# Summing four conditioning groups early, over row blocks on VectorE, instead of late on TensorE, in a hybrid decoder block

## The reference, cut to what matters

```python
c_act = jax.nn.silu(c)                                    # (1, 1024)
mod = (c_act @ w_ada + b_ada)[:, None, :]                 # w_ada is (1024, 6144)
sh1, sc1, g1, sh2, sc2, g2 = jnp.split(mod, 6, axis=-1)
h = rmsnorm(x, norm1_w) * (1.0 + sc1) + sh1
proj = h @ w_in
cq, k, v, ki, wi, rq, rf, ri, rg, gates = jnp.split(proj, IN_POINTS, axis=-1)
cq = rmsnorm(cq, q_norm_w)
q, qi = cq @ w_uq, cq @ w_uq_idx
attn = dsa_attention(q, k, v, qi, ki, wi, rel_bias)       # 256 keys a query, chosen by index scores
rec = hgrn2(rq, rf, ri, lower_bounds)                     # gated linear recurrence, 4 heads
rec = rmsnorm(rec, rec_norm_w) * jax.nn.silu(rg)
g_attn, g_rec = jnp.split(jax.nn.sigmoid(gates), 2, axis=-1)
mixed = (g_attn * (attn @ w_branch_attn) + g_rec * (rec @ w_branch_rec)) @ w_out
x = x + g1 * mixed
h2 = rmsnorm(x, norm2_w) * (1.0 + sc2) + sh2
x = x + g2 * (silu(h2 @ w_ffn_gate) * (h2 @ w_ffn_up)) @ w_ffn_down
return rmsnorm(x, final_norm_w)
```

## Time and profile before

| what | value |
|---|---|
| median of 3 runs | 1865.67 us (1864.72 to 1866.22) |
| the profiled execution's own time | 1867.28 us |
| its span (first to last instruction) | 1865.5 us |
| PE busy | 1727.7 us, 93% of the span |
| DVE busy | 822.1 us, 44% |
| ACT busy | 605.7 us, 32% |
| POOL busy | 280.9 us, 15% |
| PE's share of the chain that ended last | 75%, "issue" 13% |

### The profile page before, as it was taken

One profiled execution on the slowest core, in us unless ns is written; L12 is line 12 of the kernel. 1 busy time (PEld: TensorE's weight loads), 2 busy tenths in 40 slices (PEclk: granted clock), 3 DMA queues, 4 the chain that ended last, 5 costly groups with the idle time before them and its releaser, 6 DMA issues.

```text
span 1865.5 us, 21187 instructions
## 1 busy us (share of the span) xinstructions
PE 1727.7 (93%) x8203; PEld 1374.0 (74%) x8203; DVE 822.1 (44%) x1382; ACT 605.7 (32%) x874; POOL 280.9 (15%) x215
## 2 busy tenths in 40 slices
PE   4997899999999988999999969999999999999996
PEld 3772487888888833787877757888888888787875
DVE  4215899865574742565343462111111111234343
ACT  5235421556565412557012332111111111222232
POOL 2300122434354200223000220000000000001001
PEclk8999999999999998999999989999999999999998
DMA  9101211321122384000434311111111111342231
GB/s 323 38 26 40 62 46 46 106 64 47 56 66 65 109 319 142 1 1 5 155 118 181 130 68 46 45 45 56 45 45 52 49 45 45 124 155 93 90 124 57
DMA packets 128479, 155.28 MB, mean 83 GB/s; under 512 B 8347, under 2 KB 90390, under 8 KB 128406
## 3 DMA queue, kind: packets, MB, share of 16 engines
q1 hardware_dynamic: 119766, 135.42, 22.4%
q10 hardware_dynamic: 8064, 16.78, 2.4%
q0 software_dynamic: 576, 2.10, 0.3%
HBM read 132.77 MB, written 20.98 MB: 82 GB/s over the span
## 4 chain that ended last, share of the span: by engine, by line
PE 75%; issue 13%; DVE 4%; ACT 3%; DMA 2%; POOL 2%; SPq 1%; POOLq 0%; DVEq 0%; ACTq 0%
PE pp L496 19%; PE pp L497 18%; PE pp L498 18%; PE pp L1197 6%; PE pp L1203 3%; PE pp L1218 2%; PE pp L1386 2%; PE pp L1487 2%; PE pp L1345 2%; DMA arena<-in_w_ada 1%; DVE h_tmp L2031 1%; ACT arena L947 1%; POOL x L796 1%; PE pp L1228 0%; DVE h_raw L1699 0%
## 5 line engine op out<-in xcount | busy, mean ns | idle before, releaser
L491 DVE TENSOR_TENSOR w_lo<-raw,w_hi 128x1024 fp32r<-128x1024 f32 x112 | 140.4, 1254 | 435.5 <-ACT w_hi L486 435.5
L496 PE MATMUL pp<-h_hi,w_hi 128*128 128x512 f32 x704 | 276.3, 393 | 13.6 <-DVE h_lo L2037 13.6
L486 ACT ACTIVATE w_hi<-raw 128x1024 fp32r<-128x1024 f32 x112 | 118.5, 1059 | 522.6 <-PE pp L498 522.6
L497 PE MATMUL pp<-h_lo,w_hi 128*128 128x512 f32 x704 | 275.7, 392 | 0.0
L498 PE MATMUL pp<-h_hi,w_lo 128*128 128x512 f32 x704 | 275.5, 391 | 0.0
L496 PE MATMUL pp<-hT_hi,e_hi 128*128 128x512 f32 x416 | 168.2, 404 | 6.8 <-POOL hT_lo L694 6.0
L1745 DVE TENSOR_SCALAR_CACHE_REDUCE arena<-arena,bound 128x384 bf16<-128x384 f32 (+2 forms) x192 | 169.4, 942 | 0.8
L496 PEld LDWEIGHTS pp<-h_hi,w_hi 128*128 128x128 f32 x704 | 133.4, 189 | 42.0 <-DVE h_lo L2037 14.1
L498 PE MATMUL pp<-hT_hi,e_lo 128*128 128x512 f32 x416 | 164.3, 395 | 0.0
L497 PE MATMUL pp<-hT_lo,e_hi 128*128 128x512 f32 x416 | 164.2, 395 | 0.0
L498 PEld LDWEIGHTS pp<-h_hi,w_lo 128*128 128x128 f32 x704 | 133.4, 189 | 27.9
(11 more groups left out here) (225 smaller groups left out, 2797.1 us busy)
## 6 DMA issues: line engine op xcount, KB each, us to landing
arena<-in_w_ada SPq DMA_DIRECT2D x48, 512.0 KB, 5.0
raw<-in_w_ffn_down SPq DMA_DIRECT2D x44, 512.0 KB, 3.2
arena<-in_w_in SPq DMA_DIRECT2D x33, 512.0 KB, 3.8
raw<-in_w_ffn_gate SPq DMA_DIRECT2D x22, 512.0 KB, 3.8
raw<-in_w_ffn_up SPq DMA_DIRECT2D x22, 512.0 KB, 3.7
gates_t<-arena ACTq DMA_DIRECT2D x32, 256.0 KB, 2.1
gate_in<-gates_t SPq DMA_DIRECT2D x8, 1024.0 KB, 5.3
raw<-in_w_out SPq DMA_DIRECT2D x16, 512.0 KB, 3.4
```

The lines of the kernel that those rows point to most:

```text
L486: act.activation(w_hi[n % 2][:, :], raw[:, n % 4, :], ACT.Copy).then_inc(hi_ready, 1)
L491: dve.tensor_tensor(w_lo[n % 2][:, :], raw[:, n % 4, :], w_hi[n % 2][:, :].bitcast(F32), ALU.subtract).then_inc(lo_ready, 1)
L496: nc.tensor.matmul(out, ah, bh, start=start and k == 0, stop=False)
L497: nc.tensor.matmul(out, ah, bl, start=False, stop=False)
```

## The change

The late conditioning parts are taken out of the ring and out of their place behind the projections. They are computed as eight row blocks a part. SP loads blocks of 128 rows by 1024 columns (`late_rows`, 32 of them, 512 KB each): the first of each part straight into an accumulator `ada_acc`, the others into nine slots. DVE multiplies the first with its column of `c_act` (`TENSOR_SCALAR`) and adds the other seven (`SCALAR_TENSOR_TENSOR`), so that 128 partial sums a column lie in the 128 partitions. The biases of the gates go into the row of partition 0 (`late_bias`). Behind the index scores PE sums over the partitions: 16 matmuls with one column of ones, and four with a matrix of ones (`vrows`, set by a `memset` on DVE). ACT copies the results out, `g2` goes through DRAM and comes back to `g2_row` when `scan_gate` is free.

ACT waits for `ada_summed` 25 ahead of the evacuations of the index queries, and for 34 (all sums and both biases) ahead of the first relu. The core of the diff, by engine:

```diff
-    plan_ada(4, 12)
+    LATE_PARTS = [3, 4, 2, 5]
+    for n in LATE_STEPS:
+        if n % 8:
+            t = n - n // 8 - 1
+            s = t % 9 if t < 21 else 4 + (t - 21) % 5
+            SLOT_OF[n], STEP_BEFORE[n] = s, last_step.get(s)
+            last_step[s] = n
 # SP
-        load_from(("a", 0), ("rf", 0))
+        load_from(("a", 0), ("a", 2))
+        def late_rows(n):
+            part, k = divmod(n, 8)
+            if k and STEP_BEFORE[n] is not None:
+                sp.wait_ge(ada_summed, STEP_BEFORE[n] + 1 + (STEP_BEFORE[n] >= 24))
+            dst = ada_slot[SLOT_OF[n]] if k else ada_acc[part]
+            c0 = LATE_PARTS[part] * D
+            sp.dma_start(dst, w_ada[k * P:(k + 1) * P, c0:c0 + D]).then_inc(ada_loaded[n // 4 % 4], 16)
+        sp.wait_ge(turned_act, 8)
+        sp.wait_ge(turned_dve, 8)
+        sp.wait_ge(mod_read, 2)
+        sp.wait_ge(part_full, 4)
+        sp.wait_ge(col_full, 4)
+        for n in range(10):
+            late_rows(n)
+        ...
+        load_from(("a", 2), ("rf", 0))
+        for n in range(10, 24):
+            late_rows(n)
+        load_from(("rf", 0), "uqi")
+        for n in range(24, 32):
+            late_rows(n)
+        load("uqi")
         sp.wait_ge(pj_free, G_B + 2)
 ...
+        sp.wait_ge(cum_ready, RH)
+        sp.wait_ge(g2_stored, 16)
+        sp.dma_start(g2_row, g2_d.broadcast_to([P, D])).then_inc(gb_loaded, 16)
 ...
-        load_from(("ada", 5, 0), ("ada", 11, 3))
-        load(("ada", 11, 3))
-        sp.wait_ge(ada_done, 32)
 # ACT
+        act.wait_ge(ada_summed, 25)
 ...
+        act.wait_ge(ada_summed, len(LATE_STEPS) + 2)
 ...
+        act.wait_ge(col_full, 5)
+        act.activation(mod[:, 16:32], bank[2][:, 0:16], ACT.Copy).then_inc(mod_read, 1)
+        for r, dst in enumerate((g1_row, g2_tile)):
+            act.wait_ge(part_full, 5 + r)
+            act.activation(dst, pp[2 + r][:, :], ACT.Copy).then_inc(mod_read, 1)
+        act.wait_ge(mod_read, 5)
+        act.dma_start(g2_d, g2_tile[0:1, :]).then_inc(g2_stored, 16)
 # PE
+        pe.wait_ge(sc_relu, len(SCORED) * NIH)
+        pe.wait_ge(ada_summed, len(LATE_STEPS) + 2)
+        for i in range(16):
+            last = pe.matmul(bank[2][:, i:i + 1], ada_acc[i // 8][:, i % 8 * P:(i % 8 + 1) * P], vrows[:, 0:1], start=True, stop=True)
+        last.then_inc(col_full, 1)
+        for r in range(2):
+            for hf in range(2):
+                last = pe.matmul(bank[4 + 2 * r + hf], vrows[:, :], ada_acc[2 + r][:, hf * HALF:(hf + 1) * HALF], start=True, stop=True)
+            last.then_inc(part_full, 1)
         one_tile(("rq", 0), G_RQ0)
 ...
-        for j in range(4, 8):
-            if j >= 6:
-                pe.wait_ge(mod_read, j - 3)
-            ada_chunk(j, bank[j % 2])
-
         pe.wait_ge(lv_free, LV * RH)
-        for j in range(8, 12):
-            ada_chunk(j, bank[j - 4])
 ...
-        pe.wait_ge(grow_ready, 2)
-        pe.wait_ge(mod_read, 6)
 # DVE
+        def late_sum(n):
+            part, k = divmod(n, 8)
+            acc = ada_acc[part]
+            if n % 4 == 0:
+                dve.wait_ge(ada_loaded[n // 4 % 4], 64 * (n // 16 + 2))
+            if k == 0:
+                dve.tensor_scalar(acc, acc, c_act[:, 0:1], None, ALU.mult).then_inc(ada_summed, 1)
+            else:
+                dve.wait_ge(ada_summed, n + max(0, part - 2))
+                dve.scalar_tensor_tensor(acc, ada_slot[SLOT_OF[n]], c_act[:, k:k + 1], acc, ALU.mult, ALU.add).then_inc(ada_summed, 1)
 ...
+        for n in range(24):
+            late_sum(n)
+        late_bias(0)
         dve.wait_ge(ks_read, NT)
 ...
+        for n in range(24, 32):
+            late_sum(n)
+        late_bias(1)
 ...
-        for j in range(4, 8):
-            mod_columns(j)
-        dve.tensor_tensor(g1_row, pp[2][:, :], gb_rows[:, 0, :], ALU.add).then_inc(grow_ready, 1)
-        dve.tensor_tensor(g2_row, pp[3][:, :], gb_rows[:, 1, :], ALU.add).then_inc(grow_ready, 1)
```

More of the change, by code:

```diff
@@ L147, in build @@
     qaT = at(G0 + 10240, SEQ)
-    gb_rows = at(G0 + 11264, 2, D)
+    ada_acc = [at(G0 + o, D) for o in (6144, 7168, 9216, 10240)]
+    ada_slot = [at(o, D) for o in (F0, F0 + 1024, F0 + 2048, F0 + 3072, G0 + 4096, G0 + 5120, G0 + 8192, G0 + 11264, G0 + 13312)]
+    gate_bias = [at(E0 + 3072, D)[0:1, :], at(E0 + 384, D)[0:1, :]]
+    g2_tile = at(G0 + 6144, D)
     mask_wide = at(G0 + 13312, 8, P)
@@ L288, in build @@
     pool_step = sem("pool_step")
-    ada_done = sem("ada_done")
+    ada_summed = sem("ada_summed")
     mod_read = sem("mod_read")
@@ L334, in build @@
     rt_free = sem("rt_free")
-    grow_ready = sem("grow_ready")
+    g2_stored = sem("g2_stored")
     near_ready = sem("near_ready")
@@ L398, in build @@
     ring = Ring(4)
[L400 to L406, removed]
+    ADA_COLS = [0, D, HALF, D + HALF]
+    LATE_PARTS = [3, 4, 2, 5]
+    LATE_STEPS = [n for n in range(8 * len(LATE_PARTS))]
+    SLOT_OF, STEP_BEFORE, last_step = {}, {}, {}
+    for n in LATE_STEPS:
[4 more added lines that the diff above has]
+            last_step[s] = n
     E = {}
@@ L569, in _ @@
         sp.dma_start(bias_d, brow[:, :]).then_inc(brow_stored, 16)
-        load_from(("a", 0), ("rf", 0))
+        load_from(("a", 0), ("a", 2))
[13 more added lines that the diff above has]
+            late_rows(n)
+        for i, part in enumerate((2, 5)):
+            sp.dma_start(gate_bias[i], T["b_ada"][:, part * D:(part + 1) * D]).then_inc(gb_loaded, 16)
+        load_from(("a", 2), ("rf", 0))
[5 more added lines that the diff above has]
+        load("uqi")
         sp.wait_ge(pj_free, G_B + 2)
@@ L573, in _ @@
         sp.dma_start(kT[1][0:HD, :], kT[1][HD:P, :]).then_inc(k_copied, 16)
-        load_from(("rf", 0), ("ada", 4, 0))
+        load_from("uq", ("gate", 3, 3))
+        load(("gate", 3, 3))
+        sp.wait_ge(cum_ready, RH)
+        sp.wait_ge(g2_stored, 16)
+        sp.dma_start(g2_row, g2_d.broadcast_to([P, D])).then_inc(gb_loaded, 16)
         sp.wait_ge(pj_full, G_END)
-        load_from(("ada", 4, 0), ("ada", 5, 0))
         for i in range(2):
@@ L979, in rec_start @@
             act.wait_ge(cum_ready, h + 1)
+            if h == 0:
+                act.wait_ge(g2_stored, 16)
             a3 = cumT.rearrange("p (c t) -> p c t", t=P)
@@ L1211, in _ @@
         pe.wait_ge(cact_ready, 1)
[L1213 to L1219, removed]
         def ada_parts(j):
@@ L1419, in rec_last @@
                 last.then_inc(ro_full, 1)
+        pe.wait_ge(sc_relu, len(SCORED) * NIH)
[7 more added lines that the diff above has]
+            last.then_inc(part_full, 1)
         one_tile(("rq", 0), G_RQ0)
+        pe.wait_ge(mod_read, 5)
         pe.wait_ge(pj_free, G_RFQ[1])
@@ L1635, in _ @@
         dve.tensor_copy(vcol[:, :], bank[7][:, 0:V_END]).then_inc(vcol_ready, 1)
+        link(dve.memset(vrows[:, :], 1.0))
         dve.wait_ge(cact_ready, 1)
@@ L1666, in _, with late_bias @@
         dve.tensor_scalar(one_lb[:, :], lb[:, :], -1.0, 1.0, ALU.mult, ALU.add).then_inc(lb_ready, 1)
[L1667 to L1674, removed]
-            ins.then_inc(mod_read, 1)
-            dve.wait_ge(mod_read, j - 1)
+        def late_sum(n):
[8 more added lines that the diff above has]
+                dve.scalar_tensor_tensor(acc, ada_slot[SLOT_OF[n]], c_act[:, k:k + 1], acc, ALU.mult, ALU.add).then_inc(ada_summed, 1)
+        def late_bias(r):
+            acc = ada_acc[2 + r][0:1, :]
+            dve.wait_ge(ada_summed, 24 + 9 * r)
+            dve.wait_ge(gb_loaded, 32)
+            dve.tensor_tensor(acc, acc, gate_bias[r], ALU.add).then_inc(ada_summed, 1)
         dve.wait_ge(ident_ready, 1)
@@ L1901, in _ @@
                                      ALU.mult, ALU.subtract).then_inc(rt_lo, 1)
+        dve.wait_ge(mod_read, 5)
         link(dve.tensor_tensor(mod[:, 16:32], mod[:, 16:32], vcol[:, V_BADA + 24:V_BADA + 40], ALU.add))
```

7 lines of the change are left out of this document (2 added, 5 removed).

## The result

The changed kernel takes 1842.41 us, median of four runs (1840.36 to 1843.55), where the kernel before takes 1865.52 beside it. The ratio is 0.9878, 95% interval 0.9864 to 0.9892: 23.1 us faster. The forecast was 1832.0, in a range of 1827 to 1840. The direction was right, the gain was a third smaller than forecast, and the time lies 2.4 us above the range.

The account below looks back on a forecast made before the run. PE, busy for 93% of the span, was taken as the bound. Terms -47.8 + 0.6 + 7.7 + 2.0 + 3.8 = -33.7 us took 1867.28 to 1833.6; the runs' median, 1.6 lower, gave 1832.0, range 1827 to 1840.

Parts of the forecast that it names:

- The end: After the recurrence: without conditioning parts and their DMA waits, the bias matmuls come 47.8 us earlier.
- the wait for `on_ready`: After the recurrence: PE's transposes wait for the output norm's last product, at 670.33, leaving PE idle 18.5 us.
- the clock behind it: At the transposes after PE's idle time: eight take 2.23 us instead of 1.04, so 1.2 us is lost.
- The first stage: Under the token-major projection: 24 sums on DVE end by 113.5, in time for the norm of `cq` at 114.51.
- The rival of the slow pace: First stage: blocks come every 1.93 us, PE gets `rf` 4.5 us later, 1836.5 us; chance 0.10.
- The split of `rf`: POOL's split near 111 to 113 us, which PE awaits, is held up by DVE's adding; costs 0.6 us.
- The stall at `uqi`: Ahead of the index queries: `uqi`, issued near 131.9 behind block 31, lands at 135.8; PE stands still 7.7 us.
- The low clock behind it: Index queries after PE's pause at 128.1: matmuls first run at the 1.2 GHz level; costs 2.0 us.
- The sum matmuls: Behind the index scores: 16 one-column and four 512-column matmuls on PE's path, with a wait, cost 3.8 us.

Follow-up runs that it names:

- e9: e6 with DVE's sums 20 to 23 and the first bias moved behind the norm of `cq`; 1820.35 us, ratio 0.9768.
- e2: Changed kernel with the copies of `kT` held back until the first index product is done, `uqi` still behind the blocks; 1838.48 us, ratio 0.9860.
- e3: Changed kernel with the copies of `kT` and the tile `uq` held back until PE has begun the index queries; 1838.53 us, ratio 0.9857.
- e1: Changed kernel with `uqi` and the copies of `kT` issued ahead of the last eight row blocks; 1827.87 us, ratio 0.9803.
- e5: Changed kernel with PE's sum matmuls and ACT's copies of them moved behind the work on `rq`; 1835.68 us, ratio 0.9844.
- e10: e6 with four one-column matmuls ahead of each wide one instead of sixteen ahead of four; 1819.99 us, ratio 0.9756.
- e6: Changed kernel with the edits of e1 and e5 together; 1822.23 us, ratio 0.9764, and once more 1824.58 us, ratio 0.9781.
- e4: Changed kernel with the four wide sum matmuls ahead of the sixteen one-column ones; 1840.28 us, ratio 0.9873.
- e7: Changed kernel with 15 of the 16 one-column matmuls left out; 1833.99 us, ratio 0.9832.
- e11: Changed kernel with the edits of e1, e5, e9 and e10 together; 1821.71 us, ratio 0.9741.

## Why the prediction was wrong in size

**The end, 47.8 us.** Right: 48.0, and by the steps named, the wait for `on_ready` and the clock behind it.

**The first stage is covered.** Right: PE waits for no tile in the `a` blocks, and DVE is in time at 114.46. The rival of the slow pace is out.

**The split of `rf`, 0.6 us.** Right: 3.07 against 2.40, and e9 takes it back.

**The stall at `uqi`, 7.7 us, measured 13.7.** The first failed step. The prediction had the place, the cause and the issue time. It failed where it said that `uqi` "lands after 3.7 us alone, with block 31's bytes ahead of it a little later". Not one block but two stood in the DMA engines ahead of it, issued from 129.90 to 131.55, and the two copies of `kT` behind it came in between: 10.1 us. The prediction listed the copies as late and never as a load on the tile. Even its upper end, 10 us of stall, was too low, since it took a median landing, 5.0 us, as the worst case. e2 and e3 show the share of the copies, e1 that the whole term was avoidable.

**The low clock behind it, 2.0 us.** Right: 15.93 - 13.97 = 1.96.

**The sum matmuls, 3.8 us, measured 10.6.** The second failed step, and it has two halves. "16 one-column matmuls at 1.95 / 16 = 0.12 us are 1.95, four of 512 columns at 19.50 / 44 = 0.44 are 1.77": the counts in those rows are of records, of which each such matmul has two. The diff and the code of before would have shown it, as 64 instructions L1218 stand behind its 128 records (the prediction's "128 matmuls"). At full clock the price is 7.0 us (e5, e10); the miscount is 3.2 of the 6.8 us missed. The other 3.6 are the clock: "at the low clock it would be 7.3, but PE comes from dense work" took it that dense work before keeps the clock up during what follows. PE did not come from dense work: it was busy for 6.51 of the 8.80 us from 216.0 to 224.8. And where it did, in e6 and e9 behind `rq`, the clock fell all the same under the sixteen one-column matmuls; e4, e7 and e10 tie the fall to them.

Small terms that were not forecast took 2.3 us off. The scores took 1.0 less: before, the clock under them was 0.50 from 146 to 152 us, in the changed kernel it only dipped to 0.78 and 0.65 between 161 and 167. Behind the wait for `ri` the low clock cost 0.7 less; the 0.6 behind the bias matmuls were not looked into. With 0.7 less at the split and the start, and 0.3 at the end and behind `uqi`, the two failures, 6.0 + 6.8, leave 9.5 of the 9.6 us by which the profiled time of 1843.2 missed 1833.6; the last 0.1 is rounding.

The range failed for the same reason as the value: its bounds were taken around counts and landings that were themselves misread, and both errors were on the same side. That the time came out within 2.4 us of it is in part luck: 2.3 us came from the small terms.

## What to carry to other kernels

Where a transfer that an engine waits for is moved behind others, price its landing with all bytes that stand ahead and all that are issued right behind it, and look first whether it needs to stand there at all. Before a row's busy time is divided by its count, check the count against the number of instructions in the code. Small matmuls cost least here between wide ones and beside a wait, and an in-order engine whose instruction is moved forward takes its own waits with it.

## What the runs showed of the hardware

- A load of 512 KB issued from one queue landed in 3.7 us alone, 7.1 to 7.3 behind two others of its size, and 9.3 to 10.1 (five profiles) with two SBUF copies of 256 KB issued 0.5 and 1.1 us behind it. Those copies took 9.0 to 9.5 us there and 3.4 us when nothing else ran (e2).
- PE's clock fell to 1.2 GHz while PE was busy without a gap, under sixteen float32 one-column matmuls in a row, in nine of ten profiles that have them (all but e5; e7 has only one such matmul). It fell beside a DMA share of 0.00 (e6) and held beside 1.04 (e7). With the same matmuls mixed four to one wide one it stayed at 2.4 GHz in both profiles (e10, e11).
- One row of PE at 55 us starts up to 3.7 us apart in the profiles of the changed kernel and e1 to e11, whatever the edit, and in two groups: 53.6 to 54.4 us in six, 56.1 to 57.3 in seven. In the window from 32 to 38 us the granted clock was 1.00 in all of the first group and 0.57 to 0.86 in the second (0.54 in the profile of before). Why an execution falls in one or the other was not looked into. A difference of times taken without that offset would credit it to the edits.
